# A state-space layer in chunks of four tokens, with strips of the array side by side

## The reference, cut to what matters

```python
# 64 groups of 16 channels, 64 complex states a group, 256 steps of time
bu_re = jnp.einsum('btgc,gpc->btgp', u, bbar_re)
bu_im = jnp.einsum('btgc,gpc->btgp', u, bbar_im)
# h[t] = abar * h[t-1] + bu[t], complex and diagonal
_, _, h_re, h_im = lax.associative_scan(_complex_scan_combine, elems, axis=1)
y = (jnp.einsum('btgp,gcp->btgc', h_re, c_re) - jnp.einsum('btgp,gcp->btgc', h_im, c_im))
y = jax.nn.gelu(y + d_skip * x)
z = y @ w_glu + b_glu
return z[..., :dim] * jax.nn.sigmoid(z[..., dim:])
```

## Time and profile before

| | us |
|---|---|
| median of 3 runs | 1824.13 (1823.16 to 1824.55) |
| profiled execution | 1827.78 |
| its span | 1825.9 |
| dense gated unit, first product to last add | 328.55 to 522.4 |
| state-space scan, first drive to first output product | 531.9 to 670.4 |
| output unit | 670.4 to 728.5 |
| TensorE busy | 1705.1 (93%) |
| VectorE busy | 1386.6 (76%) |
| ScalarE busy | 960.7 (53%) |
| GpSimd busy | 125.2 (7%) |

### The profile page before, as it was taken

One profiled execution on the slowest core, in us unless ns is written; L12 is line 12 of the kernel. 1 busy time (PEld: TensorE's weight loads), 2 busy tenths in 40 slices (PEclk: granted clock), 3 DMA queues, 4 the chain that ended last, 5 costly groups with the idle time before them and its releaser, 6 DMA issues.

```text
span 1825.9 us, 33497 instructions
## 1 busy us (share of the span) xinstructions
PE 1705.1 (93%) x13898; PEld 1526.0 (84%) x13898; DVE 1386.6 (76%) x1995; ACT 960.7 (53%) x1442; POOL 125.2 (7%) x99
## 2 busy tenths in 40 slices
PE   6998798899969889699999999999999999999996
PEld 5787777899954458599999999999999999999996
DVE  5355432898859961598898888888988988988985
ACT  1323210545530001377677677676777776777774
POOL 0005100000016640000000000000000000000000
PEclk8999998899988899799999999999999999999999
DMA  7220003455440032189899899899899898898990
GB/s 295 91 92 3 4 3 117 162 182 182 169 185 1 0 134 108 50 330 359 310 348 363 305 350 362 308 356 357 305 355 340 325 357 328 330 363 310 349 341 24
DMA packets 76501, 422.45 MB, mean 231 GB/s; under 512 B 8624, under 2 KB 8880, under 8 KB 41536
## 3 DMA queue, kind: packets, MB, share of 16 engines
q1 hardware_dynamic: 75744, 418.18, 61.7%
q0 software_dynamic: 608, 2.15, 0.3%
HBM read 419.24 MB, written 1.05 MB: 230 GB/s over the span
## 4 chain that ended last, share of the span: by engine, by line
PE 82%; DVE 12%; issue 3%; ACT 2%; DMA 0%; POOL 0%; DVEq 0%; POOLq 0%; SPq 0%; ACTq 0%
PE PS L1083 32%; PE PS L1099 17%; PE PS L970 11%; PE PS L608 8%; DVE SA L1471 2%; DVE SGS L1479 2%; DVE WLO L1503 2%; PE PS L1107 2%; PE PS L957 2%; PE PS L1091 1%; PE PS L590 1%; DVE SA L1464 1%; PE PS L754 1%; DVE WLO L1508 1%; PE PS L771 1%
## 5 line engine op out<-in xcount | busy, mean ns | idle before, releaser
L1503 DVE TENSOR_TENSOR WLO<-EXA,WHI 128x1024 fp32r<-128x1024 f32 x448 | 530.2, 1221 | 88.8 <-ACT WHI L509 88.2
L1083 PE MATMUL PS<-WHI,XGH 128*128 128x256 f32 x1792 | 509.2, 284 | 3.1 <-DVE XGL L1584 2.4
L1083 PE MATMUL PS<-WLO,XGH 128*128 128x256 f32 x1792 | 507.3, 283 | 0.0
L1083 PE MATMUL PS<-WHI,XGL 128*128 128x256 f32 x1792 | 507.3, 283 | 0.0
L509 ACT ACTIVATE WHI<-EXA 128x1024 fp32r<-128x1024 f32 x448 | 450.5, 1060 | 0.0
L1083 PEld LDWEIGHTS PS<-WHI,XGH 128*128 128x128 f32 x1792 | 340.6, 190 | 12.6 <-DVE XGL L1584 2.6
L1083 PEld LDWEIGHTS PS<-WLO,XGH 128*128 128x128 f32 x1792 | 340.6, 190 | 8.0
L1083 PEld LDWEIGHTS PS<-WHI,XGL 128*128 128x128 f32 x1792 | 340.7, 190 | 0.0
L1508 DVE TENSOR_TENSOR WLO<-EXB,WHI 128x1024 fp32r<-128x1024 f32 x224 | 272.8, 1218 | 2.4 <-ACT WHI L515 2.4
L515 ACT ACTIVATE WHI<-EXB 128x1024 fp32r<-128x1024 f32 x224 | 237.0, 1058 | 8.4 <-PE PS L1099 8.4
L534 ACT ACTIVATE MSG<-PS 128x128 f32<-128x128 f32 x224 | 62.1, 277 | 268.1 <-PE PS L1083 268.1
(11 more groups left out here) (359 smaller groups left out, 2608.0 us busy)
## 6 DMA issues: line engine op xcount, KB each, us to landing
EXA<-in_wmoe SPq DMA_DIRECT2D x224, 1024.0 KB, 7.8
EXB<-in_wmoe SPq DMA_DIRECT2D x224, 512.0 KB, 5.6
FRA<-in_wffn SPq DMA_DIRECT2D x22, 1024.0 KB, 6.0
RING<-in_wsq SPq DMA_DIRECT2D x16, 1024.0 KB, 4.9
FRB<-in_wffn SPq DMA_DIRECT2D x22, 512.0 KB, 3.9
GLUW<-in_wglu SPq DMA_DIRECT2D x8, 1024.0 KB, 12.6
LORA<-in_lora SPq DMA_DIRECT2D x1, 1536.0 KB, 21.9
LORA<-in_lora SPq DMA_DIRECT2D x1, 1152.0 KB, 18.7
```

Of the source, the lines that this page charges most:

```text
L1083: mm = pe.matmul(PS[:, n % 2, 0:T], x[:, k, :], w[:, n % 2, cols], start=k == 0 and m == 0, stop=k == KC - 1 and m == 2)
L1503: tt(WLO[:, n % 2, cols], EXA[n % NSLOT][:, cols], WHI[:, n % 2, cols].bitcast(F32), ALU.subtract)\
```

## The change

The scan over 256 tokens becomes one over 64 chunks of four tokens.
- What a token gives to the three after it in its own chunk is a set of four small matrices (taps), C times the power d of the state factor times B, for d = 0 to 3; d_skip goes on the diagonal of the first. They are made during the dense gated unit (`tap_round`), and `taps` applies them.
- `drive` sums a chunk's four tokens, each with B times its own power of the factor, in PSUM. There are thus four transposed sets of B (BBT 0 to 3), made in 16 transpose rounds.
- The scan has 8 steps in place of 32: a step holds four chunks of channels with 64 chunk states each (4 x 64 = 256 columns), so the angle tables have 8 x 256 columns. MAG holds the factor to the power four, and zero at the start of each quarter.
- `read_out` multiplies the state at a chunk's start by C times powers 1 to 4 (CW 1 to 4). GpSimd forms the real and the imaginary part itself (PQ), with two more operations a step.
- In `drive`, `taps` and `read_out` consecutive products go to the four strips q of the array (32 rows, 32 columns, or both).
- The layer is done in two halves of four channel chunks. After `read_out(0)` TensorE begins the first four output tiles on half their inputs, and ends them after `read_out(1)`.
- GpSimd clears CW and BK2 when the last square weight is used. B and C come as half-size arrays. VectorE makes their scaled powers in steps 1 to 8 with six operations of 512 elements each (`complex_by`), in step 9 it adds the diagonal, and it fills the tables in steps 11 to 18, one each. ScalarE expands them into the block form with four operations at a time (`expand`), in steps 1 to 5 and 7 to 10; its sines fall in steps 16 and 20. Expert weights are sent for when `read_out(1)` is done.

The core of the diff:

```diff
+        CW = at("CW", [P, STEP + 1, 2, 32, 32], F32, r(16))
+        BK2 = at("BK2", [P, 2, 32, 32], F32, r(56))
+        BK = [CW[:, STEP], CW[:, 0], BK2[:, :, :, :]]
...
+        PQ = at("PQ", [P, NQ, 2, T], F32, 0)
...
+        ROUNDS = {4: (0, 0), 5: (0, 2), 6: (None, 0), 8: (1, 0), 9: (1, 2), 10: (2, 0), 11: (2, 2), 12: (3, 0), 13: (3, 2)}
+        TURNED = (0, 6, 10, 14)
...
+            def expand(dest, src, m, scale=1.0):
+                for h in range(2):
+                    own = slice(h * STATES, (h + 1) * STATES)
+                    act.activation(dest[own, m, :, 16 * h:16 * h + 16], src[own, m, :, :], ACT.Copy, scale=scale)\
+                       .then_inc(S("blk"), 1)
+            def turned_back(k, n):
+                act.wait_ge(S("bt_ps"), TURNED[k] + n + 1)
+                act.activation(flat(BBT[k][:, n // 2, n % 2 * 4:n % 2 * 4 + 4, :]), PS[:, 3, :], ACT.Copy).then_inc(S("bt_sb"), 1)
...
+            def between(t):
+                if t in (1, 3, 4, 5):
+                    n = (1, 3, 4, 5).index(t)
+                    if n == 0:
+                        act.wait_ge(S("zero"), 2)
+                        act.wait_ge(S("c_in"), 32)
+                    else:
+                        act.wait_ge(S("bb"), 2 + 2 * n)
+                    expand(CW[:, n], CD[n], 0)
+                    expand(CW[:, n], CD[n], 1, -1.0)
+                if t in (2, 7, 8, 10):
+                    dest, src, ready = {2: (0, 1, 2), 7: (1, 2, 12), 8: (2, 1, 14), 10: (1, 2, 16)}[t]
+                    act.wait_ge(S("bb"), ready)
+                    if t in (7, 8):
+                        act.wait_ge(S("bt_ps"), 6)
+                    elif t == 10:
+                        act.wait_ge(S("bt_ps"), TURNED[1] + 4)
+                    for m in range(2):
+                        expand(BK[dest], BD[src], m)
+                if t == 9:
+                    act.wait_ge(S("bb"), 10)
+                    act.wait_ge(S("bt_ps"), 6)
+                    expand(CW[:, STEP], CD[0], 0)
+                    expand(CW[:, STEP], CD[0], 1, -1.0)
+                if t in ROUNDS:
+                    k, n = ROUNDS[t]
+                    for x in (n, n + 1):
+                        if k is None:
+                            tap_back(x)
+                        else:
+                            turned_back(k, x)
...
+                between(t)
...
+            def turn_round(k, n):
+                done = TURNED[k] + n
+                pe.wait_ge(S("blk"), (8, 24, 28, 36)[k])
+                if done > 0:
+                    pe.wait_ge(S("bt_sb"), done)
+                for c in range(4):
+                    first = 4 * (n % 2 * 4 + c)
+                    tr = pe.transpose(PS[:, 3, c * P:(c + 1) * P], flat(BK[(0, 1, 2, 1)[k]][:, n // 2, first:first + 4, :]), ident)
+                tr.then_inc(S("bt_ps"), 1)
...
+            def tap_round(n):
+                pe.wait_ge(S("blk"), 20)
+                pe.wait_ge(S("bt_sb"), 4 + n)
+                for c in range(4):
+                    for m in range(2):
+                        for q in range(NQ):
+                            j = 4 * (4 * n + c) + q
+                            mm = pe.matmul(PS[32 * q:32 * q + 32, 3, c * P:(c + 1) * P], BK[0][:, m, j, :], CW[:, 0:STEP, m, j, :],
+                                           start=m == 0, stop=m == 1, skip_group_check=True)
+                mm.then_inc(S("bt_ps"), 1)
+            def prepare(t, x):
+                if t in ROUNDS:
+                    k, n = ROUNDS[t]
+                    if k is None:
+                        tap_round(n + x)
+                    else:
+                        turn_round(k, n + x)
...
+                prepare(t, 0)
                 if t >= 1:
                     ffn_down(t - 1)
+                prepare(t, 1)
...
+            by_step = lambda x: x.rearrange("p (n i) -> p n i", i=STEP)
+            strip = lambda q: slice(32 * q, 32 * q + 32)
+            def drive(part):
+                for cc in range(4):
+                    c = 4 * part + cc
+                    if part == 0 or cc == 0:
+                        pe.wait_ge(S("n_out"), 16 + (c + 1 if part == 0 else KC))
+                    for m in range(2):
+                        for i in range(STEP):
+                            for q in range(NQ):
+                                if part == 1 and cc == 0 and m == 0 and i == 0:
+                                    pe.wait_ge(S("s_lin"), q + 1)
+                                first = m * T + cc * CHUNKS
+                                mm = pe.matmul(PS[:, q, first:first + CHUNKS], BBT[STEP - 1 - i][strip(q), m, c, :],
+                                               by_step(HN[strip(q), c, :])[:, :, i], start=i == 0, stop=i == STEP - 1,
+                                               tile_position=(32 * q, 0), skip_group_check=True)
+                                if cc == 3 and m == 1 and i == STEP - 1:
+                                    mm.then_inc(S("bu_ps"), 1)
+            def taps(part):
+                for c in range(4 * part, 4 * part + 4):
+                    for d in range(STEP):
+                        for q in range(NQ):
+                            out = by_step(PS[strip(q), 4 + c // 2, c % 2 * T:(c % 2 + 1) * T])
+                            pe.matmul(out[:, :, d:STEP], TAP[c // 4][strip(q), c % 4, d, :],
+                                      by_step(HN[strip(q), c, :])[:, :, 0:STEP - d], start=c % 2 == 0 and d == 0, stop=False,
+                                      tile_position=(32 * q, 32 * q), skip_group_check=True)
+            def read_out(part):
+                pe.wait_ge(S("s_prod"), 16 * (part + 1))
+                for cc in range(4):
+                    c = 4 * part + cc
+                    for i in range(STEP):
+                        for m in range(2):
+                            for q in range(NQ):
+                                out = by_step(PS[strip(q), 4 + c // 2, c % 2 * T:(c % 2 + 1) * T])
+                                mm = pe.matmul(out[:, 1:CHUNKS, i], CW[:, i + 1, m, 4 * c + q, :],
+                                               PQ[:, q, m, cc * CHUNKS:(cc + 1) * CHUNKS - 1], start=False,
+                                               stop=i == STEP - 1 and m == 1, skip_group_check=True)
+                    mm.then_inc(S("yq_ps"), 1)
+            def glu_part(t, chunks, first):
+                for h in range(2):
+                    for k in chunks:
+                        if t == 0 and h == 0:
+                            pe.wait_ge(S("s_y"), k // 2 + 1)
+                        mm = pe.matmul(half(t % 4, h), GLUW[:, t, h * D + k * P:h * D + (k + 1) * P], HN[:, k, :],
+                                       start=first and h == 0 and k == chunks[0], stop=k == KC - 1, skip_group_check=True)
+                return mm
+            pe.wait_ge(S("bt_sb"), 18)
             pe.wait_ge(S("n_var"), 3)
+            drive(0)
+            pe.wait_ge(S("taps"), 2)
+            taps(0)
+            drive(1)
+            taps(1)
+            read_out(0)
+            for t in range(4):
+                pe.wait_ge(*glu_in(t))
+                pe.wait_ge(S("s_lin"), NQ + t + 1)
+                glu_part(t, range(0, 4), True)
+            read_out(1)
             for t in range(NGLU):
+                if t < 4:
+                    mm = glu_part(t, range(4, 8), False)
+                else:
+                    pe.wait_ge(*glu_in(t))
                     pe.wait_ge(S("g_mul"), t - 3)
+                    mm = glu_part(t, range(8), True)
+                mm.then_inc(S("glu_used"), 1)
...
-                    dve.wait_ge(S("s_prod"), 2 * n - 2)
+                    dve.wait_ge(S("s_prod"), 4 * n - 6)
                 for m in range(2):
-                    dve.tensor_tensor_scan(SGS[:, v, m, :], S5T[:, 7, n:n + 1].to_broadcast([P, T]), SA[:, v, m, :],
-                                           0.0, ALU.mult, ALU.add).then_inc(S("s_g"), 1)
+                    dve.tensor_tensor_scan(SGS[:, v, m, :], MAG[:, n, :], SA[:, v, m, :], 0.0, ALU.mult, ALU.add).then_inc(S("s_g"), 1)
...
+            pool.wait_ge(S("used"), NSQ)
+            pool.memset(CW[:, :, :, :, :].rearrange("p a b c d -> p (a b c d)"), 0.0).then_inc(S("zero"), 1)
+            pool.memset(BK2[:, :, :, :].rearrange("p a b c -> p (a b c)"), 0.0).then_inc(S("zero"), 1)
+            pool.wait_ge(S("trig"), 4)
+            pool.wait_ge(S("used"), NSQ + NFFN)
+            for n in range(2 * NQ):
+                v, q = n % 2, n % NQ
                 pool.wait_ge(S("s_g"), 2 * n + 2)
+                if n > 0:
+                    pool.wait_ge(S("s_prod"), 4 * n)
                 for x, trig in ((SPC, COS), (SPS, SIN)):
+                    tt(x[:, :, :], SGS[:, v, :, :], trig[:, n:n + 1, :].to_broadcast([P, 2, T]), ALU.mult).then_inc(S("s_prod"), 1)
+                if n >= NQ:
+                    pool.wait_ge(S("yq_ps"), 4)
+                pool.wait_ge(S("s_prod"), 4 * n + 2)
```

(60 more changed lines are left out.)

188 lines of the change are left out of this document (100 added, 88 removed).

## The result

| | before | changed kernel |
|---|---|---|
| median of 4 runs (us) | 1824.34 (1823.16 to 1826.23) | 1800.61 (1796.63 to 1803.02) |
| ratio, 95% interval | | 0.9853 (0.9833 to 0.9873) |
| profiled execution, span | 1827.78, 1825.9 | 1803.02, 1800.9 |
| dense gated unit | 193.8 | 245.3 |
| its last add and the norm | 9.6 | 11.1 |

What follows compares the result with a forecast made beforehand. TensorE was taken to bound the gated unit, VectorE and GpSimd taking turns the scan; -71.5 us (scan and output unit) and +43.6 (gated unit) gave -27.9, 1799.9 profiled, so 1796 us, range 1768 to 1822.

Steps and rivals of the forecast that it cites:

- first four steps: Scan stage after drive(0): turns, rotations and scans until turn 3 has emptied its bank, 13.3 us.
- second half: Scan stage after drive(1): turn 4, scan 3, GpSimd's step 3, read_out(0), its sums, steps 5 to 7; 30.7 us.
- half start: Output unit: first halves of four output tiles done under scan steps 4 to 7, 13.8 us less afterwards.
- The new wait: Gated unit: two rounds share PSUM bank 3, TensorE waits for ScalarE's copy in nine steps, +25.5 us (20 to 30).
- Tap products: Gated unit: 64 products, 128 records at 53 ns, +6.8 us, or 3.7 if the column strips overlap.
- Clock behind the stops: Gated unit: low clock after five stops of 3.7 us, +6 us (0 to 18).
- The drives: Scan stage: 256 records at 50 ns, 12.8 us for drive(0); 16 us for drive(1), with 6 us at 1.2 GHz.
- The strips load side by side: Rival, 15%: the drives are bound by 29 ns a record, 7.4 us and about 9, giving 1784 us.
- The clock stays low: Rival, 10%: short products and nine stops put TensorE at the 1.2 GHz level, +49 us, 1845 us, a slower kernel.
- Read-outs: Scan stage: 256 records at 28 ns, 7.2 us each (7.2 to 14), plus 0.8 for the activation behind read_out(1).
- The other wait: Scan stage: scan 3, step 3's products and read_out(0) stand behind drive(1); VectorE gap of some 12 us.
- The clearing: GpSimd's clearing from 316 us, at worst 33 us, costs nothing; rival, 3%: it holds VectorE back 21 us, 1817 us.

Runs made afterwards that it cites:

- e1: Changed kernel with ScalarE copying a step's first round ahead of its waits for the gated product and down products: 1756.41 us, ratio to before 0.9615.
- e2: Changed kernel with the four expansions of a step behind the two copies instead of ahead of them: 1780.32 us (one run).
- e5: Changed kernel with 16 dense products, whose result nothing reads, between taps(0) and drive(1): 1796.92 us (one run).
- e7: e1 with taps(1) moved ahead of drive(1): 1756.01 us (one run).
- e3: Changed kernel with one strip doing all its products before the next begins, in drive(1), taps(1) and read_out(1): 1836.86 us (one run).
- e8: e1 with VectorE's scan of step 3 ahead of its first products of step 4, and taps(1) ahead of drive(1): 1749.99 us (one run).
- e9: e8 with five dense products behind the last down product and eight behind the norm's sums, ahead of drive(0): 1745.84 us (one run).

## Why the prediction was right

The sign, the size and the mechanism held; most terms came within a few us, and the drives were right for a wrong reason, by luck.

| term | forecast | measured |
|---|---|---|
| drive(0) | 12.8 | 12.9 |
| first four steps | 13.3 | 12.5 |
| drive(1) | 16 | 13.6 |
| second half | 30.7 | 28.1 |
| read_out(1) | 8.0 | 5.2 |
| scan stage against 138.5 | -57.7 | -66.2 |
| half start | -13.8 | -13.8 |
| transposes, taps | +12.1 | +9.1 |
| stops | +25.5 | +30.6 |
| clock behind them | +6 | +10.4 |
| rest of the gated unit | 0 | +1.4 |
| norm, ahead of and behind the stages | 0 | +3.5 |
| sum, against the profiled execution | -27.9 | -25 |

- **The new wait** was read from the order of the two queues alone, and it is there nine times with the releaser named; e1 removes it and e2 the part that the expansions make. The four short stops have the forecast length (1.7 against 1.75). The long ones were mis-sized: an expansion of 512 elements takes 0.64 us among its neighbours, not the 0.49 I took, and step 4 had 2 us more, since the copy stands behind one more wait of ScalarE's, for VectorE's gated product.
- **Tap products**: the 128 records took 3.8 us and not 6.8, which is the lower value of the forecast, "3.7 if the column strips overlap".
- **Clock behind the stops**: mis-sized. Behind a stop of 4.3 us it costs about 2 us each time; I had taken 1.2 from one stop of 10 us and one of 3.3.
- **The drives**: right in size, wrong in kind. The step "so (0.89 - 0.19) / 15 = 47 ns apart, across strips", at clock 1.00, led me to 50 ns as the rate at the full clock and 107 ns at half. In truth this order of strips does 27 to 30 ns at 2.4 GHz (e5, e7) and 50 to 54 at 1.2, and the drives ran at 1.2. Two errors cancelled by luck, and "a clock row of 0.5 through them", which the prediction lists as a sign of being wrong, came true. The rival "The strips load side by side" named the true rate, and the rival "The clock stays low" the true clock; each alone would have been far off. The conditions under which that second rival was to turn the sign came close to true as well (both drives at 1.2 GHz, 2 us behind five of the nine stops), and the sign stayed, since a record at that level costs 50 to 54 ns and not 107. The 16 loads of the earlier trace rows belong to products of 256 columns; that this is why they stood 47 ns apart was not tried.
- **Read-outs**: 15 ns a record for 32-column tiles in four strips, where I took 28 from 64-row tiles. In one strip it is 45 (e3). With their pause a read-out is 4.9 to 5.2 us, not 7.2, and the 0.8 I added for the activation isn't on the path: TensorE goes on with the chunks that are ready.
- **The other wait**, "read_out(0) all stand behind drive(1)", is there: VectorE idle 9.69 us, where some 12 were forecast. e8 takes back 9.0 us of the stage; 5.1 of them came with the clock alone (e7).
- **The clearing** held nobody: 8.6 us for 10,240 elements, 0.84 ns each and not 2.65. By the Trainium skill, SBUF — State Buffer, Who interferes with whom, a VectorE instruction with two SBUF inputs does not contend with a GpSimd instruction that only writes SBUF; the trace agrees, with 3.26 us for VectorE's scalings beside it and 3.25 without it.

## What to carry to other kernels

When work with a single buffer is laid around another engine's stage, look at where the copy that frees the buffer stands in its engine's queue: here nine copies behind waits they had no need of cost 41.7 us (e1), more than the whole change brought, and the order of the two queues shows it before anything runs.

Price short products at both clocks, and ask which one they will get: here the drives, coming out of an idle stretch, ran at 1.2 GHz for 11 to 14 us with TensorE busy throughout. Real work moved into the idle time ahead of them (e7) gave 5.1 us by its place alone.

Let neighbours in TensorE's queue go to different strips: the same products in strip order took 2.2 to 3.2 times as long (e3).

## What the runs showed of the hardware that I had not expected

- The clock of the drives (products of 32 rows by 128 columns with 64 moving columns) went with what TensorE had done before them. After 3.4 to 5 us of idleness they ran at 1.2 GHz to their ends, 13 to 14 us at 99% busy; drive(0) of the changed kernel did so after 1.2 us at the higher level. After 11 to 13 us of other products drive(1) ran at 2.4 GHz for all of its 7.6 us (e5, and e7 with 1.4 us idle in between). In the changed kernel the taps behind drive(0) began at 1.2 GHz and had 2.4 from 600.5 on; in e9 the taps behind the quick drive(0) had a mean clock of 0.59.
- Some rows of short products at 2.4 GHz have a pause of 1.0 to 1.5 us with "issue" as the only releaser: read-outs with the clock at 1.00 throughout, after 149 to 252 records, and drive(0) of e9 after 191. drive(1) of e5 and e7, 256 records at the same level, has none, and neither has a read-out that ran mostly at 1.2 GHz (e7, 6.15 us, clock 0.58). What it is was not tried. For a read-out it takes back about half of what the higher clock gives, 5.2 us against 6.2.
- GpSimd's sum of 256 elements takes 0.72 us alone and 1.1 beside VectorE's work on two SBUF inputs; VectorE's scan of 256 takes 1.26, 1.75 or 2.72 us for its two instructions, by what GpSimd does at the time. A step of the scan is 5.1 us while both are at it (GpSimd's first products at 603.18, 608.26 and 613.34 in the changed kernel) and 4.0 when GpSimd is alone (e8: its step 7 from 594.87 to 598.90).
